# A seven-product 2x2 block scheme for 32 k-tile pairs of each feed-forward layer of a decoder trunk

## The reference

```python
def swiglu_ffn(x, norm_pre, w_gate, w_up, w_down, norm_post):
    h = rms_norm(x, norm_pre)
    a = jax.nn.silu(jnp.einsum('bsd,df->bsf', h, w_gate)) * jnp.einsum('bsd,df->bsf', h, w_up)
    y = jnp.einsum('bsf,fd->bsd', a, w_down)
    return x + rms_norm(y, norm_post)        # d = 2048, f = 5632
```

## Time and profile before

| | |
|---|---|
| median of 3 runs | 2012.21 us (2011.69 to 2015.17) |
| the profiled execution | 2011.53 us, span 2009.8 us |
| busy PE, DVE, ACT, POOL | 1988.8, 1182.1, 1033.4, 200.3 us |
| matmuls | 9802 |
| granted TensorE clock, mean | 0.996 |
| DMA | 407.59 MB, mean 203 GB/s |

### The profile page before, as it was taken

How to read it: one execution, slowest core, us unless ns; L and a number is a source line. 1 busy time by engine, 2 the same in 40 slices (tenths; PEclk the granted TensorE clock), 3 DMA queues, 4 the chain that set the end, 5 groups by cost and what they waited for, 6 DMA issues and landing times.

```text
span 2009.8 us, 27715 instructions
## 1 busy us (share of the span) xinstructions
PE 1988.8 (99%) x9802; PEld 1688.0 (84%) x9802; DVE 1182.1 (59%) x1457; ACT 1033.4 (51%) x1280; POOL 200.3 (10%) x124
## 2 busy tenths in 40 slices
PE   9999999999999999999899999999999999999998
PEld 7898888888888888888899988888888888888886
DVE  5755565555555554444599985655555555554544
ACT  6544464545455443434788865554444444444433
POOL 1000000000000000000589940000000000000000
PEclk9999999999999999999999999999999999999999
DMA  9645566666666675555455535576666666665554
GB/s 337 226 147 189 173 217 226 216 220 213 215 213 219 221 220 196 191 197 191 139 189 180 187 118 199 167 236 214 213 217 220 217 220 218 213 215 191 197 190 145
DMA packets 137968, 407.59 MB, mean 203 GB/s; under 512 B 15330, under 2 KB 38498, under 8 KB 137378
## 3 DMA queue, kind: packets, MB, share of 16 engines
q1 hardware_dynamic: 135796, 396.84, 59.8%
q0 software_dynamic: 2096, 9.70, 1.3%
HBM read 392.84 MB, written 13.63 MB: 202 GB/s over the span
## 4 chain that ended last, share of the span: by engine, by line
PE 98%; DVE 1%; ACT 0%; POOL 0%; issue 0%; DMA 0%; DVEq 0%; SPq 0%; ACTq 0%; POOLq 0%
PE acc L1390 84%; PE acc L1401 4%; PE acc L1403 4%; PE acc L1402 4%; PE acc L1654 0%; PE acc L1442 0%; PE acc L1440 0%; DMA raw<-in_units 0%; PE acc L1632 0%; PE acc L1640 0%; ACT xT_hi L784 0%; DVE acc L959 0%; PE acc L1499 0%; DVE xT_lo L987 0%; PE acc L1501 0%
## 5 line engine op out<-in xcount | busy, mean ns | idle before, releaser
L946 DVE SCALAR_TENSOR_TENSOR w_lo<-raw,vecs,w_hi 128x1024 fp32r<-128x1024 f32 x398 | 509.1, 1282 | 438.1 <-ACT w_hi L582 437.9
L582 ACT ACTIVATE w_hi<-raw,vecs 128x1024 fp32r<-128x1024 f32 x398 | 457.9, 1152 | 514.3 <-PE acc L1390 478.2
L582 ACT ACTIVATE w_hi<-raw 128x1024 fp32r<-128x1024 f32 x304 | 321.8, 1059 | 363.3 <-PE acc L1390 350.4
L944 DVE TENSOR_TENSOR w_lo<-raw,w_hi 128x1024 fp32r<-128x1024 f32 x236 | 288.7, 1225 | 315.6 <-ACT w_hi L582 315.6
L1390 PE MATMUL acc<-w_hi,xT_hi 128*128 128x512 f32 x1528 | 472.2, 390 | 0.6 <-DVE xT_lo L987 0.6
L1390 PE MATMUL acc<-w_lo,xT_hi 128*128 128x512 f32 x1528 | 470.5, 389 | 0.0
L1390 PE MATMUL acc<-w_hi,xT_lo 128*128 128x512 f32 x1528 | 470.4, 389 | 0.0
L1390 PEld LDWEIGHTS acc<-w_hi,xT_hi 128*128 128x128 f32 x1528 | 285.7, 188 | 62.1 <-issue 1.8
L1390 PEld LDWEIGHTS acc<-w_lo,xT_hi 128*128 128x128 f32 x1528 | 286.8, 188 | 59.8
L1390 PEld LDWEIGHTS acc<-w_hi,xT_lo 128*128 128x128 f32 x1528 | 286.8, 188 | 59.6
L1390 PE MATMUL acc<-w_lo,hT_hi 128*128 128x512 f32 x704 | 217.5, 389 | 0.0
(11 more groups left out here) (184 smaller groups left out, 1534.1 us busy)
## 6 DMA issues: line engine op xcount, KB each, us to landing
raw<-in_units SPq DMA_DIRECT2D x702, 512.0 KB, 4.2
hid_turned_blocks<-tok SPq DMA_DIRECT2D x44, 256.0 KB, 2.6
tok<-hid_turned_blocks SPq DMA_DIRECT2D x176, 64.0 KB, 2.7
gpost<-in_post POOLq DMA_DIRECT2D x4, 1024.0 KB, 6.7
x<-in_x POOLq DMA_DIRECT2D x4, 512.0 KB, 10.2
c_raw<-in_consts POOLq DMA_DIRECT2D x4, 512.0 KB, 7.8
out<-x SPq DMA_DIRECT2D x8, 256.0 KB, 2.8
xT_raw<-in_xT SPq DMA_DIRECT2D x3, 512.0 KB, 6.6
```

Of the source, the lines that this page charges most:

```text
L582: nc.scalar.activation(w_hi[:, s, :], raw[:, s, :], ACT.Copy, scale=scale).then_inc(hi_ready, 1)
L944: ins = nc.vector.tensor_tensor(w_lo[:, s, :], raw[:, s, :], w_hi[:, s, :], ALU.subtract)
L946: ins = nc.vector.scalar_tensor_tensor(w_lo[:, s, :], raw[:, s, :], vecs[:, gain:gain + 1], w_hi[:, s, :], ALU.mult, ALU.subtract)
```

## The change

In some pairs of k-tiles the 2x2 block product (two token tiles and two k-tiles of x; two k-tiles and two column halves of the weights) is made of seven products with sums and differences of the blocks in place of eight. These are the units of slots 0 and 1 of quads 1 and 2 in the chunks 1 to 9, of quads 4 to 9 in the first half of the down projection and of quads 2 to 9 in the second. The blocks of x are summed once per layer (`sum_rows` by DVE, `hi_rows` by ACT, `lo_rows` by DVE), those of the weights for each pair: `sum_units` by DVE ahead of the splits, then a high part by ACT and a low part by DVE (`split_fast`). Four of the products go into banks of their own, across all pairs of a chunk or half (`shared_bank`, the 4 banks that the next chunk uses); the others into the usual ones. After the last pair ACT copies one of these banks and DVE combines them (`keep_first`, `add_parts`), and at the end of the chunk DVE adds them to the usual sums (`close`; in the last half `fold`, before the end, with PE's last units in another order: token 0's and token 1's units up to slot 1 of the last quad, then slots 2 and 3 of each token). Where blocks of x are summed, the norm's gain can't be in the weights: for k-tiles 4 to 15 it is now applied when the turned x is copied (`hi_xT`, `lo_xT`, four instructions in place of one). The loops over chunks and quads are written out on all engines, some tensors share other places in SBUF, and POOL's load of the post-norm gains waits for the last gate/up sum. What is not shown: ACT's order in `ffn`, which is DVE's (each `hi_rows` of the down projection stands after quads 0, 1 and 2, ahead of the next quad's splits), the new semaphores and tensors, PE's loops with waits for them, and the new opening.

```diff
+FAST_QUADS = (1, 2)
+FAST_CHUNKS = range(1, FFC - 1)
+FAST_DOWN = (range(4, 10), range(2, 10))
+DOWN_PAIRS = 8
+SUM_BATCHES = ((0, 3), (3, 6), (6, 8))
+GATE_SUMS = len(FAST_QUADS) * len(FAST_CHUNKS)
+        def private_bank(z, t, h):
+            return 4 * z + 2 * t + h
+        def shared_bank(z, n):
+            return 4 * (1 - z) + n
...
+                def split_fast(q, n, raw_sum):
+                    act.wait_ge(raw_sum_ready, n)
+                    split(q, 0)
+                    split(q, 1)
+                    if n > 1:
+                        act.wait_ge(sums_used, n - 1)
+                    nc.scalar.activation(sum_hi[:], raw_sum, ACT.Copy).then_inc(sum_hi_ready, 1)
+                    split(q, 2)
+                    split(q, 3)
+                def keep_first(n, z, dst, kept):
+                    act.wait_ge(sums_used, n)
+                    nc.scalar.activation(dst[:, 0, :], acc[:, shared_bank(z, 0), :], ACT.Copy).then_inc(first_kept, 1)
...
+                def hi_rows(n, dst, src):
+                    act.wait_ge(rows_ready, n)
+                    nc.scalar.activation(dst, src, ACT.Copy).then_inc(rows_hi_ready, 1)
...
+                rows = (1 + len(SUM_BATCHES)) * layer
+                for i in range(1, FFC):
+                    z = par if i % 2 == 0 else 1 - par
+                    q = i * 4 + q0
+                    for s in range(3):
+                        split(q, s, gain + s)
+                    if i - 1 in FAST_CHUNKS:
+                        kept = closing(layer, i - 2)
+                        for t in range(T):
+                            wait_sum(dve, t, gu0_ready, i + 11 * layer, q - 1)
+                            close(kept, 1 - z, parts, t, 0)
+                    split(q, 3, gain + 3)
+                    if i == 1:
+                        lo_rows(rows + 1, xs_lo[:], gate_raw_sum.rearrange("p (a c) -> p a c", c=BANK), xs_hi[:])
+                        dve.wait_ge(x_rs_ready, 2 * (e - 1) + 4)
+                    if i - 1 in FAST_CHUNKS:
+                        for t in range(T):
+                            close(kept, 1 - z, parts, t, 1)
+                        dve.wait_ge(closed, closed_count(layer, i - 1))
+                    hidden(i - 1, 0)
+                    hidden(i - 1, 1)
                     turn_hidden(i - 1, 0)
                     turn_hidden(i - 1, 1)
+                    fast = FAST_QUADS if i in FAST_CHUNKS else ()
+                    if 1 in fast:
+                        dve.wait_ge(rows_lo_ready, rows + 1)
+                        sum_units(q + 1, gate_sum(layer, i, 1), gate_raw_sum)
+                    for c in range(1, 4):
+                        if c in fast:
+                            split_fast(q + c, gate_sum(layer, i, c), gate_raw_sum, gate_sum_lo[:])
+                        else:
+                            split_quad(q + c)
+                        if c == 2:
+                            lo_hid(i - 1, 0)
+                            lo_hid(i - 1, 1)
+                        if c + 1 in fast:
+                            sum_units(q + c + 1, gate_sum(layer, i, c + 1), gate_raw_sum)
+                    if fast:
+                        add_parts(gate_sum(layer, i, fast[-1]), closing(layer, i - 1), z, parts)
...
+                for j in range(2):
+                    z = par if j else 1 - par
+                    parts_of = last_parts if j else first_parts
+                    for c in range(FFC):
+                        q = qd + j * FFC + c
+                        last_fast = FAST_DOWN[j][-1]
+                        if c in FAST_DOWN[j]:
+                            split_fast(q, down_sum(layer, j, c), down_raw_sum[:], down_sum_lo[:])
+                        elif j == 0 and 1 <= c <= len(SUM_BATCHES):
+                            a0, a1 = SUM_BATCHES[c - 1]
+                            split(q, 0)
+                            lo_rows(rows + c + 1, hs_lo[:, a0:a1, :],
+                                    down_raw_sum[:, 0:(a1 - a0) * BANK].rearrange("p (a c) -> p a c", c=BANK), hs_hi[:, a0:a1, :])
+                            for s in range(1, 4):
+                                split(q, s)
+                        elif c == FFC - 1:
+                            split(q, 0)
+                            split(q, 1)
+                            add_parts(down_sum(layer, j, last_fast), closing(layer, CLOSED - 2 + j), z, parts_of)
+                            if j:
+                                dve.wait_ge(parts_ready, closing(layer, CLOSED))
+                                for h in range(2):
+                                    fold(z, 1, h)
+                                dve.wait_ge(token0_paused, layer + 1)
+                                for h in range(2):
+                                    fold(z, 0, h)
+                            split(q, 2)
+                            split(q, 3)
+                        else:
+                            split_quad(q)
+                        if j == 0 and c == 0:
+                            hidden(FFC - 1, 0)
+                            hidden(FFC - 1, 1)
+                            turn_hidden(FFC - 1, 0)
+                            turn_hidden(FFC - 1, 1)
+                        if j == 0 and c == 2:
+                            lo_hid(FFC - 1, 0)
+                            lo_hid(FFC - 1, 1)
+                        if j == 0 and c < len(SUM_BATCHES):
+                            a0, a1 = SUM_BATCHES[c]
+                            k = 4 * (FAST_DOWN[1][0] + a0)
+                            dve.wait_ge(hT_lo_ready, 22 * layer + 20)
+                            dve.wait_ge(rows_lo_ready, rows + c + 1)
+                            sum_rows(down_raw_sum[:], first_tiles(hT_hi, k, a1 - a0), first_tiles(hT_lo, k, a1 - a0), a1 - a0)
+                        if j == 1 and c == 0:
+                            for t in range(T):
+                                wait_sum(dve, t, y0_ready, 2 * e + 1, qd + FFC - 1)
+                                for h in range(2):
+                                    close(closing(layer, CLOSED - 2), 1 - z, first_parts, t, h)
+                        if j == 1 and c == 1:
+                            gain_y(e, par, 0, (0, 1))
+                            gain_y(e, par, 1, (0, 1))
+                        if c + 1 in FAST_DOWN[j]:
+                            dve.wait_ge(rows_lo_ready, rows + 1 + len(SUM_BATCHES))
+                            sum_units(q + 1, down_sum(layer, j, c + 1), down_raw_sum[:])
...
+            def sum_rows(raw_sum, hi, lo, n):
+                r = raw_sum[:, 0:n * BANK].rearrange("p (a c) -> p a c", c=BANK)
+                a11, a21, a12, a22 = [r[:, :, i * P:(i + 1) * P] for i in range(4)]
+                after(nc.vector.tensor_tensor(r, hi, lo, ALU.add))
+                after(nc.vector.tensor_tensor(a22, a21, a22, ALU.subtract))
+                after(nc.vector.tensor_tensor(a21, a11, a21, ALU.subtract))
+                after(nc.vector.tensor_tensor(a11, a22, a11, ALU.subtract))
+                nc.vector.tensor_tensor(a12, a11, a12, ALU.add).then_inc(rows_ready, 1)
+            def lo_rows(n, dst, raw_sum, hi):
+                dve.wait_ge(rows_hi_ready, n)
+                dve.wait_ge(rows_ready, n)
+                nc.vector.tensor_tensor(dst, raw_sum, hi, ALU.subtract).then_inc(rows_lo_ready, 1)
...
+                def sum_units(q, n, raw_sum):
+                    if n > 1:
+                        dve.wait_ge(sum_lo_ready, n - 1)
+                    for s in range(2):
+                        dve.wait_ge(raw_landed[s], landings(q, s) * 16)
+                    b11, b12, b21, b22 = [raw[:, s, h * BANK:(h + 1) * BANK] for s in range(2) for h in range(2)]
+                    t3, t2, t4 = [raw_sum[:, n * BANK:(n + 1) * BANK] for n in range(3)]
+                    after(nc.vector.tensor_tensor(t3, b12, b22, ALU.add))
+                    nc.vector.tensor_tensor(t2, t3, b11, ALU.add).then_inc(dve_step, 1)
+                    steps[0] += 1
+                    nc.vector.tensor_tensor(b12, b11, b12, ALU.add)
+                    dve.wait_ge(dve_step, steps[0])
+                    nc.vector.tensor_tensor(t4, t2, b21, ALU.add).then_inc(raw_sum_ready, 1)
+                def split_fast(q, n, raw_sum, sum_lo):
+                    split(q, 0)
+                    split(q, 1)
+                    dve.wait_ge(sum_hi_ready, n)
+                    nc.vector.tensor_tensor(sum_lo, raw_sum, sum_hi[:], ALU.subtract).then_inc(sum_lo_ready, 1)
+                    split(q, 2)
+                    split(q, 3)
+                def add_parts(n, kept, z, dst):
+                    dve.wait_ge(sums_used, n)
+                    dve.wait_ge(first_kept, kept + 1)
+                    q6, q7, q5 = [acc[:, shared_bank(z, i), :] for i in (1, 2, 3)]
+                    after(nc.vector.tensor_tensor(dst[:, 1, :], q6, dst[:, 0, :], ALU.add))
+                    after(nc.vector.tensor_tensor(dst[:, 2, :], q7, dst[:, 1, :], ALU.add))
```

(29 more changed lines are left out.)

332 lines of the change are left out of this document (226 added, 106 removed).

## The result

The changed kernel takes 2035.95 us (median) against 2011.95 of the kernel before, measured on the same chip: a ratio of 1.0116, 95% interval 1.0102 to 1.013. It is slower by 24 us. The prediction said 2037, with a chance of 0.76 for slower. Three of the changed kernel's four executions took 2035.35 to 2036.27 us and one, in a slow state, 5059.82; the ratio and the profile are of the fast ones.

What follows compares the result with a forecast made beforehand. PE, busy 99% of the span, was taken to bound the kernel. Saving 43.5 us of matmuls against 18 + 14.4 + 1.8 + 12 + 13.2 + 6.5 + 3 of costs gave +25.4, about 2037 us, range 2020 to 2055.

Steps and rivals of the forecast that it cites:

- first pairs: Gate/up chunks: late DVE-ACT-DVE hand-over stalls PE 0.8 plus 0.2 us in 18 chunks, 18 us; chunk 1's row sums add 1.8.
- second pairs: Gate/up chunks: sums wait for slot 1's raw load; 0.8 us in each of 18, 14.4 us, ends 0 and 25.
- three quads at the start of a down projection: Row sums and ACT's copy ahead of the next splits stall PE 6.0 us per down projection, 12 us.
- fast quads in a row: Down projections: slot 1's load lands late, 0.75 us excess a quad less entry reserve; 13.2 us, ends 0 and 32.
- last folds: End of down projections: the last fast pair's adds and folds end 1.1 us after PE wants them, twice.
- start of the conv layer: Token 0 is ready only 2.72 us ahead of PE's end, before 5.44, lengthening PE's idle time: +2.7 us.
- end of the program: Token 0's adds run until 2.0 us after PE's end, where token 1's square started 0.4 before: +1.6 us.
- openings: Two openings: gains on turned x take 0.5 us more on ACT and DVE per token; 1.5 each, 3 us.
- Rival 4: Clock: six 2 us waits at down-projection starts drop PE to 1.2 GHz, 22 us, 2059 us; chance 0.02.
- Rival 1: Faster: DVE-ACT hand-overs in fast quads are covered, so the gate/up chunks cost nothing; 1990 us; chance 0.16.
- Rival 2: No change: savings and stalls cancel, landings at 3.2 to 4.0 us throughout; 2012 +- 4 us; chance 0.08.
- Rival 3: Landing-bound throughout: raw loads cost +45 to +55 us, 2057 to 2067 us; chance 0.10.

Runs made afterwards that it cites:

- run 1: Changed kernel with the four weight-sum adds of a fast chunk's first pair moved ahead of DVE's last closes, hiddens and transposes: 2016.27 us, ratio 1.0023.
- run 6: Changed kernel without making the weight-block sums in all 64 fast pairs (adds, ACT's copy, DVE's low part), same PE matmuls: 1992.51 us, ratio 0.9894.
- run 4: Changed kernel with 7/8 of slot 1's load left out in second pairs and in down projections from their fourth quad on: 2010.78 us, ratio 1.0001.
- run 5: Changed kernel with the same four weight-sum adds reordered, the one needing only slot 0 ahead of the wait for slot 1's load: 2018.69 us, ratio 1.0026.
- run 2: Changed kernel with ACT's row-sum copy and DVE's low part behind the next quad's slot 0 and 1 splits at down-projection starts: 2019.74 us, ratio 1.0048.
- run 3: Changed kernel with POOL's first two conv-layer splits moved behind its four roots, away from DVE's adds: 2031.09 us, ratio 1.0097.
- run 7: Changed kernel with weight sums ahead of closes, row-sum copy behind splits, POOL's splits behind roots, second-half squares and gains between splits: 1992.52 us, ratio 0.9903.
- run 9: Changed kernel with fast pairs in only one of nine gate/up chunks per layer, silu and hidden banks by chunk parity: 2034.70 us, ratio 1.0115.
- run 8: Changed kernel with all five moves: sums before closes, later row-sum copy, later POOL splits, gains between splits, slot 0's add first: 1978.99 us, ratio 0.9829.
- run 10: Version with all five order moves, but fast pairs in only one gate/up chunk per layer: 2000.00 us, ratio 0.9944, against 1978.99 with nine chunks.

## Why the prediction was right, and where its terms were off

The prediction had +25.4 against the profiled execution before, and the spans of the two traces differ by 24.1. Term by term, predicted and read (from the stage lengths above and the gaps):

| term | predicted | read |
|---|---|---|
| matmuls saved | -43.5 | -43.5 (192 fewer) |
| first pairs, with the extra in chunk 1 | 18 + 1.8 | 18.8 |
| second pairs | 14.4 | 6.6 by lengths, 8.0 by gaps |
| three quads at the start of a down projection | 12 | 12.7 |
| fast quads in a row | 13.2 | 13.4 |
| last folds | 2.2 | 3.2 |
| start of the conv layer | 2.7 | 6.9 |
| clock in the conv layer's pause | 0 | 1.8, in this execution |
| end of the program | 1.6 | 1.6 |
| openings | 3 | 2.6 |
| sum | +25.4 | about +24 |

The gate/up stages grew by 2.0 in all and save 24.5, of which 1.1 belongs to the openings' later waits (0.58 + 0.87 where there were 0.29, 0.22 and 0.37, twice): 25.4 us of costs. Of these 16 x 0.95 + 2 x 1.82 = 18.8 are first pairs and 6.6 is left for the second ones. The down projections grew by 10.3 and save 19.0: 29.3, less 12.7 at their starts (6.37 twice) and 3.2 for the last folds (1.62 and 1.60), leaves 13.4 for the fast quads. The gaps there, read one by one, come to 3.4, 4.7, 3.0 and 3.7, together 14.8; the two readings differ by 1.4, and neither is surer.

**First pairs.** The chain was timed almost to the hundredth: sum at 6.24 and DVE's split at 9.96 by the prediction, 6.26 and 9.96 in the trace; PE's stall 0.8 + 0.2 predicted, 0.95 read. The 0.2 for the low part of the sums is not a term of its own: the weight loads wait 0.2 for it 36 times, and the lengths of the stages have no room for it. The reserve of 10.45 and the prices of the earlier trace rows were good, and run 1 shows that the mechanism is the one named.

**Second pairs.** This is the term that failed most, 14.4 against 6.6 to 8.0. (The second pair begins 10.41 to 11.04 us after the first, where run 6 has 10.20: 7.1 in all.) I had read the landing times right (median 4.2 after as before) and then given half of the pairs 5.4, from one burst of loads at 282 us. In the timeline above slot 1's split ends at 396.62 and the load lands at 401.02: 4.4 less 0.16 for the issue is 4.2, for which the prediction's own sum has a stall between 0.05 and 0.4. The outlier should have been an end of the range and not half of the mean.

**Down projections.** 2.25 + 0.1, 2.0 and 1.6 were predicted, 2.40, 2.13 and 1.84 read: 0.05, 0.13 and 0.24 low. The chain of the first came out as predicted: the row sums took 4.09 us (736.57 to 740.66), and DVE's split ended 12.65 behind its time 0, for 12.7. Why the third is 0.24 longer no run shows. The fast quads in a row mostly follow each other by 10.2 to 11.1, three of them by 11.25 to 12.1: DVE's own round is 10.1 (797.68 to 808.62 is 10.94, with a wait of 0.83 for the load in it), which is the number of the prediction, and the rest is landing, as it said and as runs 4 and 5 show. What it did not see is that the entry's reserve depends on the waits before: run 2 got 3.5 us in addition.

**Conv layer.** Token 0's later readiness was seen (+2.7), and it is there. What was missed is the place of y: half of it is kept in SBUF now, and POOL's split of the next weights runs at that time. Twice 2.1 us on DVE, shown by run 3. The prediction has no term for it: the change moves an operand of these adds from PSUM to SBUF, and the question of who else uses SBUF then was not asked.

**The clock.** In the profiled execution of the changed kernel the conv layer's pause, from the end of PE's wait for POOL (2.28 us before, 2.30 after) to the next weight products, took 21.9 us in place of 20.1, because PE ran at half of its clock (1.2 GHz) from its start on. The pause in windows (us, busy time and instructions of each engine, granted clock, DMA share, GB/s), before, after, and in run 1:

```profile
1168.97:1189.10 20.13, 17.78 (x91) 15.56 (x91) 14.11 (x41) 10.41 (x21) 7.62 (x5) 0.83 0.28 109
...
1183.20:1205.20 22.00, 20.57 (x91) 18.49 (x91) 14.14 (x41) 10.43 (x21) 7.65 (x5) 0.69 0.26 98
...
1173.70:1193.90 20.20, 17.83 (x91) 15.62 (x91) 14.17 (x41) 10.46 (x21) 7.67 (x5) 0.83 0.32 109
```

This is not a cost of the change. With the same matmuls the pause took 20.1 us in runs 1, 2, 3, 4, 5 and 7 as well, 21.9 to 22.0 in runs 6 and 9, and 20.6 to 20.7 in runs 8 and 10. What decides it these traces don't show; the term of 1.8 belongs to one execution.

Rival 4, that the waits of 2 us at the starts of the down projections lower the clock, came true in part and cost nothing. The first quads of layer 0's and of layer 1's down projection behind their waits of 2.40 us, and layer 1's next wait:

```profile
744.50:747.50 3.00, 2.92 (x13) 2.38 (x14) 3.00 (x3) 1.53 (x2) 0.00 (x0) 1.00 0.54 175
1793.80:1797.20 3.40, 3.37 (x8) 2.65 (x9) 3.40 (x3) 1.46 (x2) 0.00 (x0) 0.53 0.47 154
...
1806.70 0.30 PEld L1646 LDWEIGHTS acc<-w_hi,hT_hi 128*128 128x128 f32 x2 [0.56 <-issue]
```

In layer 0 the granted clock stayed at 1.00; in layer 1 it was about half for 3.4 us. But the next quad begins 12.90 us later in both, since it waits for DVE's low part: the slower PE only made its next wait shorter, 0.56 in place of 2.13. All seven kernels with these waits (the changed one and runs 1, 3, 4, 5, 6 and 9) show one such fall, behind one of their two waits of 2.40; the four without them (2, 7, 8 and 10) show none. The clock also stood at 0.50 from 984 to 988 us, behind the 7.54 us wait at the conv layer's start, where it was 1.00 before. The stalls of 0.95 didn't lower it (1.00 from 290 to 730 us). The prediction's price for the clock, 22 us, did not appear. The rule that it takes from the Trainium skill ("TensorE: Matmul & The Clock Gate", HAM oscillation) describes a kernel with longer waits for each k-tile; the trace agrees with it behind some of the longer waits here, and to apply it to the short ones of the gate/up chunks was the prediction's own step.

**The rivals.** Rival 1 (the hand-overs are covered) fell: each was over its limit by what the sum said. Rival 2 (savings and stalls cancel) fell with the 24 us. Rival 3 (5.4 throughout) fell with the second pairs. Rival 4 is answered above. No rival's time was right. The mechanism of the forecast holds, but that its sum is so near is partly luck: the failed terms (-6.4 to -7.8, +4.2, +1.8, +1.0) cancelled largely; the 1.3 us between forecast and result is better than the terms are.

## What to carry to other kernels

Before an engine with 40% idle time gets new work, write down the chain of hand-overs that must fit between the freeing of a buffer and its next use: here 0.7 us over a limit of 10.45 took 0.95 of the 1.36 us that a fast chunk saved, and nearly the same instructions in another order gave it back (2036 to 1979 us, with PE, DVE and ACT at about the same work). Start the chain that another engine waits for first, and put what nobody waits for soon (closes, transposes, copies) behind it. Where a step waits for two buffers, do first what needs only the one that lands earlier. When an operand moves from PSUM to SBUF, look at what POOL does at that time. And since the clock alone made the same stage 1.8 us longer in some traces than in others, read a stage in several traces before giving it a cause.

## What the runs showed of the hardware

- DVE's add of 512 elements with both inputs in SBUF took 0.71 us with POOL idle; two of them took 3.5 beside one POOL TENSOR_TENSOR of 2.36 us (128 x 1024, SBUF to SBUF). With one input in PSUM it was 0.70, and 0.68 beside such a POOL instruction (four in 2.73 in the kernel before).
- A raw load of 512 KB landed after a median of 4.2 us, before and after the change. DVE waited 20.5 us for such loads at the sums of the down projections; with 7/8 of slot 1's loads cut off it was 1.7, and with all bytes loaded but one add moved ahead of the wait it was 4.3.
- Seven products of three matmuls, each into one bank, ran at the rate of plain units: 45 matmuls in 10.20 us, and 442 or 443 plain ones in 100.
- The same stretch of small matmuls (the conv layer's pause) took 20.1, 20.7 or 21.9 us in different traces, at a mean granted clock of 0.83, 0.75 or 0.69.
